# The first norm's shift as row products on TensorE, two blocks of w_in by tiles, and the modulation products spread differently over the later stages

## What is computed

```
c_act = silu(c)                                  # one vector of 1024
ada = c_act @ w_ada + b_ada                      # 1024 x 6144
sh1, sc1, g1, sh2, sc2, g2 = split(ada, 6)       # six vectors of 1024
h = rmsnorm(x, norm1_g) * (1 + sc1) + sh1        # first norm, modulated
z = h @ w_in                                     # 1024 x 2560
... two causal convolutions, a gated linear recurrence (lru), head norms ...
x = x + g1 * (y @ w_out)
h = rmsnorm(x, norm2_g) * (1 + sc2) + sh2        # second norm
x = x + g2 * peer(h, ...)                        # expert layer, most of the time
```

## Time and profile before

| | |
|---|---|
| median of 3 runs | 2641.67 us (2639.65 to 2642.42) |
| the profiled execution | 2639.72 us, of which span 2638.4 us |
| busy share of the span | TensorE 96%, its weight load 78%, VectorE 55%, ScalarE 34%, GpSimd 31% |
| HBM traffic | 311 MB read, 69 MB written |

### The profile page before, as it was taken

The page is one execution under the profiler, slowest core; times in us unless marked ns, Lnnn a source line. Parts: engine busy times, 40 slices in busy tenths (PEclk is TensorE's granted clock), DMA queues, the critical chain, the costliest instruction groups (busy, mean ns, idle before and its releaser), DMA issues.

```text
span 2638.4 us, 29743 instructions
## 1 busy us (share of the span) xinstructions
PE 2540.8 (96%) x11430; PEld 2067.9 (78%) x11430; DVE 1459.4 (55%) x2679; ACT 884.3 (34%) x1277; POOL 807.0 (31%) x508
## 2 busy tenths in 40 slices
PE   2998999999999999999999999999999889999998
PEld 2776778888888888888888888888877767888887
DVE  6884398676764443345655555554743656433332
ACT  4433332333333333232333333334343543322221
POOL 5434227777777730000000000004412542111100
PEclk9988999999999999999999999999998989999999
DMA  7666456666666654345464545433252122322332
GB/s 256 211 205 202 128 162 137 141 139 166 149 171 142 178 160 177 130 156 220 157 226 160 219 157 223 159 106 113 89 144 72 64 75 77 96 90 94 94 102 76
DMA packets 185795, 384.21 MB, mean 146 GB/s; under 512 B 47060, under 2 KB 112724, under 8 KB 178104
## 3 DMA queue, kind: packets, MB, share of 16 engines
q1 hardware_dynamic: 143256, 316.89, 37.0%
q0 software_dynamic: 42400, 65.42, 10.0%
HBM read 311.02 MB, written 69.34 MB: 144 GB/s over the span
## 4 chain that ended last, share of the span: by engine, by line
PE 83%; DVE 2%; ACT 1%; issue 1%; SPq 0%; DMA 0%; POOL 0%; ACTq 0%; DVEq 0%
PE bank L464 25%; PE bank L460 25%; PE bank L461 25%; PE bank L601 2%; DVE prob_lo L1294 1%; PE bank L750 1%; PE bank L752 1%; PE bank L479 0%; PE bank L478 0%; PE bank L477 0%; PE bank L751 0%; PE bank L720 0%; PE bank_stat L486 0%; ACT scaled L1176 0%; PE bank L736 0%
## 5 line engine op out<-in xcount | busy, mean ns | idle before, releaser
L460 PE MATMUL bank<-h_lo,weights_hi 128*128 128x512 f32 x2368 | 951.1, 402 | 39.6 <-ACT weights_hi L819 31.3
L461 PE MATMUL bank<-h_hi,weights_hi 128*128 128x512 f32 x2368 | 942.8, 398 | 0.0
L464 PE MATMUL bank<-h_hi,weights_lo 128*128 128x512 f32 x2368 | 605.3, 396 | 1.9 <-DVE weights_lo L1252 1.9
L819 ACT ACTIVATE weights_hi<-weights_raw 128x1024 fp32r<-128x1024 f32 (+1 forms) x411 | 430.8, 1049 | 440.0 <-PE bank L464 326.0
L460 PEld LDWEIGHTS bank<-h_lo,weights_hi 128*128 128x128 f32 x2368 | 449.1, 190 | 151.0 <-ACT weights_hi L819 34.7
L1252 DVE TENSOR_TENSOR weights_lo<-weights_raw,weights_hi 128x1024 fp32r<-128x1024 f32 (+1 forms) x346 | 436.9, 1263 | 222.3 <-ACT weights_hi L819 207.1
L464 PEld LDWEIGHTS bank<-h_hi,weights_lo 128*128 128x128 f32 x2368 | 446.0, 189 | 112.0 <-DVE weights_lo L1252 3.7
L461 PEld LDWEIGHTS bank<-h_hi,weights_hi 128*128 128x128 f32 x2368 | 449.3, 190 | 105.5 <-issue 0.2
L1951 POOL DMA_INDIRECT expert_coefs<-share,place_at x256 | 436.8, 1706 | 189.9 <-issue 85.9
L1446 DVE SCALAR_TENSOR_TENSOR residual<-bank,ada,residual 128x512 f32<-128x512 f32 x136 | 102.2, 751 | 324.7 <-PE bank L464 324.6
L1005 ACT ACTIVATE hidden<-bank 128x512 f32<-128x512 f32 x128 | 76.5, 598 | 490.9 <-PE bank L464 445.3
(11 more groups left out here) (363 smaller groups left out, 2606.0 us busy)
## 6 DMA issues: line engine op xcount, KB each, us to landing
weights_raw<-in_expert_u SPq DMA_DIRECT2D x128, 512.0 KB
weights_raw<-in_expert_v SPq DMA_DIRECT2D x128, 512.0 KB
weight<-expert_coefs POOLq DMA_DIRECT2D x16, 2048.0 KB, 8.6
hidden_store<-hidden SPq DMA_DIRECT2D x26, 1024.0 KB
hidden<-hidden_store POOLq DMA_DIRECT2D x13, 2048.0 KB, 14.1
ada_raw<-in_w_ada SPq DMA_DIRECT2D x40, 512.0 KB, 5.2
expert_coefs<-zeros SPq DMA_DIRECT2D x32, 512.0 KB, 6.1
expert_coefs<-stage SPq DMA_DIRECT2D x16, 1024.0 KB
```

The source lines that it names most:

```text
L460: M.matmul(bank[:], hi[:, c:c + P], m_lo[k], start=start and i == 0, stop=False)
L461: M.matmul(bank[:], hi[:, c:c + P], m_hi[k], start=False, stop=False)
L464: ins = M.matmul(bank[:], lo[:, c:c + P], m_hi[k], start=False, stop=stop and i == len(tiles) - 1)
L819: S.activation(w_hi[n % SPLIT][:, 0:w], w_raw[n % RAW][:, 0:w], ACT.Copy).then_inc(*hi_done.inc(n))
```

## The change

The modulation's first eight output tiles (the shift of the first norm) are now laid out in rows: c is a column of 8 x 128 (`c_column`), TensorE multiplies it with 512 outputs at a time (`shift_row`, plain float32, one output row), ScalarE copies the row to SBUF (`row_copy`) and four tiny matmuls turn it into columns (`shift_columns`), once for each half; VectorE adds the bias (`shift1`). The tiles of shift and scale arrive in a new order (`ADA_ROWS`). GpSimd's and ScalarE's part in the modulation is gone, and the squares of x are added by VectorE, so that the sum has 4 matmuls instead of 8. Blocks 0 and 1 of w_in are done together, tile by tile of h. The remaining 32 tiles of w_ada stand elsewhere: two instead of three after each convolution tile of the recurrence, none in `conv_tile(0)` and `(1)`, more among the head norms, and in the output loop 3 in pass 0 and 2 in each of passes 1 to 6, with their loads listed in the same pass of SyncE's queue.

```
-        ADA_ORDER = [j for k in range(KD) for j in (8 + k, k)] + list(range(16, 48))
+        ADA_ROWS = {0: 0, 1: 1, 3: 2, 4: 3, 8: 4, 9: 5, 11: 6, 12: 7}
...
+            def shift_row(half, js, at):
+                for j in js:
+                    b = ADA_ROWS[j]
+                    M.wait_ge(*ada_landed[ada_slot(j)][j])
+                    for n in range(2):
+                        k = 2 * (b % 4) + n
+                        ins = M.matmul(at[0:1, :], c_column[:, k:k + 1], ada_raw[ada_slot(j)][:, n * 512:n * 512 + 512],
+                                       start=k == 0, stop=k == KD - 1)
+                    ins.then_inc(*pe.inc(("ada", j)))
+
+            def shift_columns(half):
+                M.wait_ge(*act["ada_row", half])
+                for q in range(4):
+                    at = ROWS_AT + 4 * half + q
+                    ins = M.matmul(stat_bank[:, at:at + 1], ada_row[0:1, half, q * P:(q + 1) * P], const("ones")[0:1, 0:1],
+                                   start=True, stop=True)
+                ins.then_inc(*pe.inc(("ada_columns", half)))
...
+            for k in range(KD):
+                for done in ready(k):
+                    M.wait_ge(*done)
+                for i, bank in enumerate(together):
+                    if k == 0:
+                        M.wait_ge(*hi_done[i])
+                    M.matmul(bank[:], w_hi[i][:, k * P:(k + 1) * P], h_lo[:, k, :], start=k == 0, stop=False)
+                    M.matmul(bank[:], w_hi[i][:, k * P:(k + 1) * P], h_hi[:, k, :], start=False, stop=False)
...
-                for j in range(3):
-                    ada_tile(16 + 3 * c + j)
+                for j in range(2):
+                    ada_tile(16 + 2 * c + j)
...
             def conv_tile(c):
-                ada_tile(28 + 3 * c)
                 conv_mult(c)
-                ada_tile(29 + 3 * c)
                 conv_gate(c)
-                ada_tile(30 + 3 * c)
...
             for k in range(KD):
                 add_to_x(k, ("out", k), ("x1", k), ada[:, 16 + k:17 + k])
-                for j in ((40, 41) if k == 0 else (41 + k,) if k < 7 else ()):
+                for j in range(34 + 2 * k if k else 33, min(36 + 2 * k, 48)):
                     ada_tile(j)
...
             for k in range(KD):
                 load_weights(BLOCK_AT["w_out", k] + 5)
                 store_zeros()
-                for j in ((44, 45) if k == 0 else (45 + k,) if k < 3 else ()):
+                for j in range(34 + 2 * k if k else 33, min(36 + 2 * k, 48)):
                     load_ada(j)
```

More of the change, by code:

```diff
@@ L49 @@
 RING = 4
+N_EARLY = 16
+ROW_BLOCKS = 8
+ROWS_AT = 256
+TOGETHER = 2
 HEAD_SUMS = 16
@@ L508, in tensor @@
+            M.wait_ge(*dve["x_added", KD - 1])
+            sums("x_sum", [x_parts[0]], 0)
+            row = [take(("ada_row", half)) for half in range(2)]
+            M.wait_ge(*act["c_column"])
+            shift_row(0, rows[0:2], row[0])
             M.wait_ge(*dve["x_rstd"])
             spread("x_spread", 0)
-            for i in range(8):
-                product(("in", i), i, h_hi_tiles, h_lo_tiles, h_ready("h1") if i == 0 else None)
+            shift_row(0, rows[2:4], row[0])
+            pe.also(("ada_row", 0), ("ada", rows[3]))
@@ new lines, in tensor @@
+            shift_row(1, rows[4:6], row[1])
+            shift_columns(0)
+            shift_row(1, rows[6:8], row[1])
+            pe.also(("ada_row", 1), ("ada", rows[7]))
+            shift_columns(1)
+            ready = h_ready("h1")
+            together = [take(("in", i)) for i in range(TOGETHER)]
+            for k in range(KD):
[6 more added lines that the diff above has]
+                    M.matmul(bank[:], w_hi[i][:, k * P:(k + 1) * P], h_hi[:, k, :], start=False, stop=False)
@@ L512, in tensor @@
+            for i, bank in enumerate(together):
+                M.wait_ge(*lo_done(i))
+                for k in range(KD):
+                    ins = M.matmul(bank[:], w_lo[i][:, k * P:(k + 1) * P], h_hi[:, k, :], start=False, stop=k == KD - 1)
+                ins.then_inc(*pe.inc(("in", i)))
+                block_over[i] = ("in", i)
+            for i in range(TOGETHER, 8):
+                product(("in", i), i, h_hi_tiles, h_lo_tiles)
             M.wait_ge(*gate_w_landed["gate_w"])
@@ L1396, in vector @@
                 lru_output(c)
-            conv_tile(2)
+            conv_mult(2)
+            ada_tile(24)
+            conv_gate(2)
+            ada_tile(25)
+            ada_tile(26)
             def head_rstd(tiles):
@@ L2053, in sync @@
                 load_weights(2 * c + 6)
-                for j in range(3):
-                    load_ada(20 + 3 * c + j)
+                for j in range(2):
+                    load_ada(20 + 2 * c + j)
             for i in range(8, 20):
```

154 lines of the change are left out of this document (91 added, 63 removed).

## The result

The changed kernel takes 2654.16 us (median of 6 runs, 2650.15 to 2659.22); the kernel before took 2641.4 us beside it (6 runs, 2637.48 to 2644.35). The ratio is 1.0050, with a 95% interval of 1.0036 to 1.0065: slower by 0.5%. The prediction said 2644.5, a range of 2631 to 2656, and "within 0.2%" as the likeliest side. The time lies in the range and on the other side of the 0.2% line, which had been given 0.39.

The account below looks back on a forecast made before the run. TensorE, busy 96% of the span, bounds the kernel, so only its idle and slow time can be won. 11 + 1 - 15 = -3 on 2639.72 gives 2642.7; 1.95 more for the median gives 2644.5 us, range 2631 to 2656.

Parts of the forecast that it names:

- within 0.2%: Whole kernel: time no more than about 0.2% (5.3 us) from the kernel before; chance 0.41.
- Term 1, the start: From x's arrival to block 2 of w_in: row products and paired blocks end at 56.3, before 67.50; gain 11 us.
- row products at full clock from 20.3 on: Shift's row products at the start: TensorE at low speed until 20.3 us, high from there.
- row products at 1.2 GHz throughout: Rival on the start: low clock makes the shift ready at 46.8, not 34.3; gain 1.5, time 2654; chance 0.22.
- every low part in the chain is paid in full: Start, VectorE's chain: GpSimd's three low parts of weights cost 6 to 7 us, not 3; gain 7, not 11.
- Term 2, the middle: Recurrence and head norms: last y tile 2.2 us earlier, 1 charged among the head norms; gain 1, bounds -2 and +5.
- Term 3, the output loop: Output loop: tiles loaded in the pass that uses them land late, so two passes take 15.4 us, not 11.2; loss 15.
- 5.6 + 8.5 + 1.3 = 15.4: Output loop, two passes: addition to load of weights, then second tile's landing, then VectorE's work on it, in us.
- 16; I take 15, since the DMA queue is partly empty: Output loop: last addition at 265.6 instead of 249.78, a loss of 16 us, lowered to 15.
- x's last addition no longer waits for TensorE but for DMA: End of the output loop: cover gone, the last addition waits for tile loads; no separate size.
- VectorE's extra tile fits: 0.66 + 2 x 1.3 = 3.3 us in a pass of 5.6: Output loop: VectorE has time for an addition and two tiles, 3.3 us, in each pass of 5.6 us.
- tiles land in time: Rival on the output loop: passes stay at 5.6 us, the loop costs 2 to 3, time 2632.5; chance 0.17.

Follow-up runs that it names:

- run 8: Changed kernel with only block 0 of w_in in step with the first norm's tiles, block 1 an ordinary product behind it: 2652.52 us, ratio 1.0039.
- Run 2: Kernel before with only the changed kernel's places for tiles 16 to 47, on VectorE and in SyncE's list: 2663.26 us, ratio 1.0080.
- runs 3, 4 and 5: Changed kernel, in order: output-loop tile loads one pass earlier, 2645.44 us; tile loads ahead of the zeros' store, 2647.75; zeros' stores moved out of the loop, 2649.41.
- runs 9 and 10: 46 repeated matmuls (10.7 us) among the experts, added to the new start with old tile places, 2643.36 us, and to the kernel before, 2654.10 us.
- run 6: Changed kernel with output-loop tile loads one pass earlier and the zeros' stores moved out of the loop: 2639.15 us, ratio 0.9993.
- run 7: Kernel of run 6 with VectorE's output-loop tiles reading 64 of 1024 columns, all loads kept: 2632.07 us, ratio 0.9970.

## Why the prediction was right or wrong

**Term 1, the start: right in size, behind the row products partly by luck.** x times gain was put at 22.4 and came at 22.66, the end of the pair of blocks at 56.3 and came at 57.07; gain 11, measured 10.4. The choice on which most hung, row products at full clock from 20.3 on, held: the earlier trace rows were the right rows to read it from. The rival "row products at 1.2 GHz throughout" falls by the records of 22.49. Behind them two misses cancel. VectorE's chain was put at 48.7 and ended at 51.4: the two low parts of weights that fell into it cost 2.1 and 2.2 us (2.31 and 2.38 for an instruction that takes 0.22), not 3 together, and the shift came at 30.5, not 29.8. So tile 4 reached TensorE at 49.53 and not at 46.7. But all 32 matmuls from there ran at full speed, 7.5 us and not 9.6: TensorE had 12 matmuls in a row at half speed from 42.69 on, heaped up while it waited for block 1's split, and was at full speed again by 47.95. The wait for the splits, 5.8 us, no term had. Of the reading by the Trainium skill's page "SBUF — State Buffer", section "SBUF: two separate sides", under which every low part in the chain is paid in full, the trace bears out nearly all (2.1 and 2.2 of GpSimd's 2.35 and 2.37); the third low part came at 53.00, behind the chain. What this term never did was to price its second part by itself: by run 8 the pair is 1.2 us of the 10.4.

**Term 2, the middle: +1, measured about 0, and -1.5 in the profiled execution.** Run 2, with the old start, shows both halves of it, in the last y tile of the recurrence and in a wait of TensorE among the head norms:

```profile
161.62 0.69 DVE L1384 TENSOR_TENSOR y<-y,lru_x 128x512 f32<-128x512 f32 x1
```

```profile
196.44 1.13 PE L495 MATMUL bank<-consts,a_square 128*128 128x128 f32 x8 [2.58 <-ACT a_square L927]
```

The y tile comes 2.7 us earlier than 164.33, where 2.2 was predicted, and the first addition at 215.01, 0.2 later than before. So the tiles taken out of the convolution gained, and those put among the head norms cost 2.9, where the prediction charged 1. With the new start, in runs 3, 4 and 5, whose code up to there is nearly the same, the first addition stands at 204.20 to 204.33, 10.5 us ahead, and in the changed kernel's own profile at 205.90.

**Term 3, the output loop: right mechanism, too small by a quarter.** The prediction's chain is there row by row, from addition over GpSimd to the load and the landing, in two beats. It was put at "5.6 + 8.5 + 1.3 = 15.4" for two passes; the row-read pieces measured 5.2 + 8.8 + 2.5 = 16.5. The step that failed is the 8.5: it was taken as the landing of the second tile, with one tile left to do, and 8.8 was the landing of the first, so that both tiles of VectorE stood behind it. The three beats from addition 1 to addition 7 took 15.2, 16.5 and 17.3; in the last a tile beside GpSimd's low parts took 2.73. TensorE lost 7.1 us to late low parts, near the 8 that the prediction put, and as it said they were covered. The loss by this way of counting was "16; I take 15, since the DMA queue is partly empty", and it was 18.6; the discount had no row behind it and went the wrong way. The DMA share of the loop was 0.65 of a pass before; in the changed kernel seven waits of up to 5.7 us stood for tiles.

Left out of the sum was what TensorE's idleness leaves behind: 1.6 us of sums at half clock after 11.5 us without work. The prediction had named the wait ("x's last addition no longer waits for TensorE but for DMA") and not its price on the clock.

**The sum.** 10.4 - 1.5 - 18.6 - 1.6 and about 1 that comes back before the end of the experts make -10.4 by the end of the experts, where -3 was predicted: 7.4 of the 9.7 us by which the forecast was low. The rest is the difference of the medians (12.8) over that of the openings (10.4). It lies in later stages, whose length differs between the six profiles by up to 12 us; runs 9 and 10 speak against their position as the cause, and what moves medians by 2 to 5 us against their openings, either way, is left open.

**The cause of the loop's loss, which the prediction took for one thing, is two.** The late issue: 8.9 us (run 3), 8.8 without zeros (run 6 against 5). VectorE's work on two tiles a pass, where it meets GpSimd's low parts: 6.5 us (42.3 to 35.8, run 7). The zeros' traffic: 2.3. The prediction held that "VectorE's extra tile fits: 0.66 + 2 x 1.3 = 3.3 us in a pass of 5.6". That sum leaves out GpSimd, which works 3.83 of those 5.6 us. In the steady passes of run 6 it holds all the same, since they take 5.57 to 5.59 us with two tiles; but GpSimd is then full and late, and the price comes due in the last two passes, 5.8 us over 5.60 each, in a tile that lands late and in three small instructions that wait for GpSimd. For the rival "tiles land in time" with its 2632.5 run 6 is the nearest, with the loads early and the traffic light: it stands at 2639.15. It is no full test, since VectorE still waited 5.2 us for tiles there.

## What to carry to other kernels

When work is moved into a loop, ask three things of it and not one: whether its engine has room, whether the load can be issued without the loop's own chain in front of it, and whether another engine, with which it takes turns, is busy in the room that seems free. Look at the last pass by itself: a steady pass can hide a delay that the end of the loop pays. And where the profile names an engine that was long done as what ended a wait, look for what really finished just before. A load issued in the pass that uses it turns a chain of short steps into the beat of the loop. And parts of a change that gain and lose are best timed apart before they are put together: here the start alone is faster (0.9979) and the whole is slower (1.0050).

## What the runs showed of the hardware

- Products with one output row ran at either speed of TensorE. The eight records from 15.22, behind 13.5 us without work and 1.8 us of sums, took 6.25 us, and the four from 22.49 took 1.88: the speed doubled while TensorE did nothing else, and stayed through the later ones.
- It was at half speed again by 37.79, after waits of 0.68 and 2.05 us with eight tiny matmuls between them, and the granted clock from 37.7 to 47.9 is 0.50: the 14 matmuls that start there are mostly 0.43 us apart.
- Instructions on 8 columns of VectorE, 0.10 us each where GpSimd is idle (259.07 in the changed kernel), had a mean of 1.53 us beside GpSimd's low parts in run 6 (4.59 for three); the excess is larger than that of a tile 128 times their size (1.79 against 1.22).
- The same 870 us of work took 867 to 879 in six executions, by the granted clock. Executions of one kernel lie up to 14.5 us apart (run 7), so the total of a single profile does not decide between kernels whose medians differ by a few us; the times of named instructions in the opening agree to 1 to 3 us.
